# A gated tile moved behind the second pointwise product, and pairs of column sums with more buffers, in a two-block kernel

## What is computed

```python
hl = modulate(rms_norm_2(xl, norm1_g[i]), sh1_l, s1_l)
# conformer_conv(hl, rows, ...):
u = h @ w_pw1 + b_pw1
a, gate = jnp.split(u, 2, axis=-1)
u = a * jax.nn.sigmoid(gate)
u = dwconv(u.reshape(B * n_seg, L // n_seg, D), w_dw).reshape(B, L, D) + b_dw
u = jax.nn.silu(layer_norm(u, ln_g, ln_b))
yl = u @ w_pw2 + b_pw2
# second_block goes on:
xl = xl + g1_l * yl
xl = xl + g2_l * sq_relu_mlp(modulate(rms_norm_2(xl, norm2_g[i]), sh2_l, s2_l), mlp_w1[i], mlp_w2[i])
return rms_norm_2(xl, final_g)
```

## Time and profile before

| what | value |
|---|---|
| three runs | 2130.7, 2130.88 and 2135.11 us, median 2130.88 us |
| the profiled execution's own time | 2129.87 us |
| its span | 2128.1 us |
| PE busy | 2044.6 us (96%), 10322 matmuls, mean granted clock 0.98 |
| DVE busy | 1064.0 us (50%) |
| ACT busy | 814.7 us (38%) |
| POOL busy | 773.2 us (36%) |

### The profile page before, as it was taken

How to read it: one execution, slowest core, us unless ns; L and a number is a source line. 1 busy time by engine, 2 the same in 40 slices (tenths; PEclk the granted TensorE clock), 3 DMA queues, 4 the chain that set the end, 5 groups by cost and what they waited for, 6 DMA issues and landing times. The chain is left out here.

```text
span 2128.1 us, 26521 instructions
## 1 busy us (share of the span) xinstructions
PE 2044.6 (96%) x10322; PEld 1713.7 (81%) x10322; DVE 1064.0 (50%) x1881; ACT 814.7 (38%) x1365; POOL 773.2 (36%) x449
## 2 busy tenths in 40 slices
PE   9999999999999799999899987999999999999997
PEld 7988988988987588888788776778878888888886
DVE  7255445545563456553779969992423221112125
ACT  5533332254335413222456564643335333322311
POOL 3411111121113444344168956753334444222220
PEclk9999999999999899999999998998999999999998
DMA  4301101110113487673344422222233333111112
GB/s 170 108 21 54 47 21 60 41 55 26 46 46 115 164 306 267 226 267 119 109 175 181 178 74 65 83 86 70 79 89 99 95 95 98 50 50 42 48 50 79
DMA packets 69564, 215.64 MB, mean 101 GB/s; under 512 B 7856, under 2 KB 8240, under 8 KB 69312
## 3 DMA queue, kind: packets, MB, share of 16 engines
q1 hardware_dynamic: 55472, 188.26, 26.5%
q10 hardware_dynamic: 13968, 25.70, 3.6%
HBM read 184.56 MB, written 29.36 MB: 101 GB/s over the span
## 5 line engine op out<-in xcount | busy, mean ns | idle before, releaser
L1358 PE MATMUL B<-HB,WH 128*128 128x512 f32 x2976 | 943.7, 403 | 28.1 <-DVE GA L2070 15.6
L2577 POOL TENSOR_TENSOR WL<-RAW,WH 128x1024 fp32r<-128x1024 f32 x205 | 495.5, 2421 | 956.7 <-ACT WH L1755 956.2
L1358 PEld LDWEIGHTS B<-HB,WH 128*128 128x128 f32 x2976 | 552.9, 191 | 150.4 <-issue 19.4
L1358 PE MATMUL B<-HB,WL 128*128 128x512 f32 x1488 | 571.2, 394 | 5.6 <-POOL WL L2577 5.6
L1755 ACT ACTIVATE WH<-RAW 128x1024 fp32r<-128x1024 f32 x205 | 215.6, 1055 | 510.8 <-DMA RAW<-wall 491.6
L1358 PEld LDWEIGHTS B<-HB,WL 128*128 128x128 f32 x1488 | 282.7, 190 | 68.0 <-POOL WL L2577 7.2
L2073 DVE SCALAR_TENSOR_TENSOR RES<-B,modv,RES 128x512 f32<-128x512 f32 x144 | 104.9, 746 | 208.5 <-PE B L1537 182.2
L2073 DVE SCALAR_TENSOR_TENSOR B<-UP,vec,B 128x512 f32<-128x512 f32 x308 | 207.2, 747 | 0.0
L1537 PE MATMUL B<-HIDH,WH 128*128 128x512 f32 x512 | 187.7, 400 | 6.4 <-DVE HIDL L2070 4.9
L1537 PE MATMUL B<-HIDH,WL 128*128 128x512 f32 x512 | 183.6, 392 | 0.0
L1537 PE MATMUL B<-HIDL,WH 128*128 128x512 f32 x512 | 183.4, 391 | 0.0
(11 more groups left out here) (241 smaller groups left out, 2579.1 us busy)
## 6 DMA issues: line engine op xcount, KB each, us to landing
RAW<-wall SPq DMA_DIRECT2D x204, 512.0 KB, 3.5
MODRAW<-wmod ACTq DMA_DIRECT2D x96, 256.0 KB, 4.8
WH<-parts SPq DMA_DIRECT2D x32, 512.0 KB, 3.2
WL<-parts SPq DMA_DIRECT2D x32, 512.0 KB, 4.2
RES<-xT SPq DMA_DIRECT2D x16, 512.0 KB, 8.3
oscr<-OT SPq DMA_DIRECT2D x32, 256.0 KB, 2.1
OI<-oscr SPq DMA_DIRECT2D x16, 512.0 KB, 5.0
parts<-WH SPq DMA_DIRECT2D x16, 512.0 KB, 5.3
```

Source lines behind the costliest of these rows:

```text
L1358: i = pe.matmul(bank, a[:, ks], hb(part, k, h), start=k == 0 and n == 0, stop=k == 7 and n == 2)
L2577: po.tensor_tensor(lo, raw, hi.bitcast(F32), ALU.subtract).then_inc(sig[f"w_lo{q % NW}"], 1)
```

## The change

There are four edits.

1. The last gated tile of half 1, `pa` and `pg` of f = 7, leaves its place before `pw2` of half 0 and comes after it; `before_mlp(0)` now steps in the background of `pg`. The `glu` of (6, 1) and its convolution come after the first layer norm, that of (7, 1) after the MLP's norm, and the POOL convolution of (5, 1) after that.
2. In `normed(0)` the column sums are put on PE two after each group, and all of them count from the first square (`made[0]`). In `normed(1)` one sum is followed by at least one step.
3. The squares have six buffers in half 0 and eight in half 1. `LATE` of half 1 is 14.0 and not 22.0, `LATE_SQ` of half 1 is 6.0 and not 12.0.
4. From the first `ysub` of half 0 to `ln_r` the POOL lane is held, so that no tap stands ahead of the power on POOL.

```diff
-LATE, LATE_SQ, LATE_ROW = (8.0, 22.0), (5.0, 12.0), 5.0
+LATE, LATE_SQ, LATE_ROW = (8.0, 14.0), (5.0, 6.0), 5.0
...
-        for f in range(8):
+        for f in range(8 - h):
             plan += [("pa", f, h), ("pg", f, h)]
...
-    plan += [("pw2", f, 0) for f in range(8)] + mlp[0]
+    plan += [("pw2", f, 0) for f in range(8)] + [("pa", 7, 1), ("pg", 7, 1)] + mlp[0]
...
-            while lanes[lane] and now[lane] < now["pe"] + ahead[0]:
+            while lanes[lane] and now[lane] < now["pe"] + ahead[0] and not (held[0] and lane == "pool"):
...
+        held[0] = h == 0
         for f in range(8):
             piece("ysub", f, h)
             piece("ysq", f, h)
             made.append(now["dve"])
         for f in range(8):
-            yield from until(made[f] + LATE_SQ[h])
+            yield from until(made[f if h else 0] + LATE_SQ[h])
             piece("ysum", f, h)
-            if f % 2:
+            if f % 2 or h:
                 yield
         piece("ln_r", h)
+        held[0] = False
...
+            if (f, h) == (BY_POOL[1][1], 1):
+                piece("glu", f, h)
+            elif (f, h) != (6, 1):
+                convolve(f, h)
...
     hurry[0] = False
+    convolve(6, 1)
...
     second_product(0)
-    beside(before_mlp(0), {0: 1, 1: 1, 2: 1, 3: 1, 4: 1})
+    while not up_free[5]:
+        lanes_step()
+    product("pa", 7, 1)
+    bg.append(before_mlp(0))
+    product("pg", 7, 1)
+    drain()
+    convolve(7, 1)
+    lane_add("pool", conv_pool(BY_POOL[1][1], 1))
     first_hidden(0)
...
-        YT = [[at(f"YT{h}{i}", 512, F32, (x0 + (10 + i) * K2, hb0 + (4 + i) * K4 + K2)[h]) for i in range(4)] for h in range(2)]
+        YT = [[at(f"YT0{i}", 512, F32, x0 + (10 + i) * K2) for i in (0, 1, 2, 3, 6, 7)],
+              [at(f"YT1{i}", 512, F32, hb0 + (4 + i) * K4 + K2) for i in range(8)]]
...
-                if f >= 4:
-                    w.wait_ge(sig["ysum"], nth["ysum", f - 4, h] - h)
-                ac.activation(YT[h][f % 4][:, :], CO[h][f][:, :], ACT.Square).then_inc(sig["ysq"], 1)
+                n = len(YT[h])
+                if f >= n:
+                    w.wait_ge(sig["ysum"], nth["ysum", f - n, h] - h)
+                ac.activation(YT[h][f % n][:, :], CO[h][f][:, :], ACT.Square).then_inc(sig["ysq"], 1)
```

More of the change, by code:

```diff
@@ L183, in make_plan @@
     lanes = {"dve": [], "pool": []}
-    ahead, pace = [AHEAD], [PASS]
+    ahead, pace, held = [AHEAD], [PASS], [False]
     def u_split():
@@ L871, in make_plan, with convolve @@
     piece("a2")
+    def convolve(f, h):
+        piece("glu", f, h)
+        if f in BY_POOL[h]:
+            lane_add("pool", conv_pool(f, h))
+        else:
+            lane_add("dve", conv_dve(f, h))
     for h in range(2):
-        for f in range(8):
+        for f in range(8 - h):
             while not up_free[(8 * h + f) % 10]:
@@ L1633, in ysum @@
                 for t in range(4):
-                    i = pe.matmul(bank[:, t:t + 1], YT[h][f % 4][:, t * 128:(t + 1) * 128], ones[:, 0:1],
+                    i = pe.matmul(bank[:, t:t + 1], YT[h][f % len(YT[h])][:, t * 128:(t + 1) * 128], ones[:, 0:1],
                                   start=f == 0 and t == 0, stop=f == 7, skip_group_check=True)
```

## The result

The changed kernel takes **2115.76 us** (median of 4 runs, 2112.25 to 2117.7) where the kernel before takes 2132.95 in the same session: ratio 0.9927, 95% interval [0.9913, 0.9941]. Five more runs in a later session gave 2116.39 and 0.9937 [0.9925, 0.9949]. By the two ratios it is faster by 13 to 16 us; the forecast was 2126.0 with a range down to 2119, so the direction was right and the size was not. The profiled execution of the changed kernel has a span of 2115.9 us, 12.2 shorter than before.

A forecast was written before the change was run, and what follows sets the result against it. PE was taken as the bound, busy 2044.6 of 2128.1 us, with DVE setting the end of `pw2`. Gains 0.6 + 2.6 + 1.7 = 4.9 us took the profiled 2129.87 to 2125.0, median forecast 2126.0, range 2119 to 2134.

The forecast's parts named there:

- The first layer norm: Half 0's sums: half clock from the third pair, last sum at 1241.8 as before, row at 1247.7, not 1249.23.
- The case of the full clock: Rival: clock holds in half 0's sums, row at 1242.7, 9.8 us gained, 2121.1 us; chance 0.23.
- "slower" rival: Clock falls at half 0's first pair, normalised tiles 4.2 us later; half 1 loses another 5.7; 2135.9 us; chance 0.15.
- The fall at 1478: Clock drop at half 1's sums in the earlier trace, taken as agreeing that frequent micro-idles can lower the clock.
- Normalised tiles, `pw2`, the MLP's norm: Steps after half 0's row: last low part at 1261.6, `pw2` ends 44.5 us later, norm gap 25.4; 2.6 us kept.
- Z: Moment the last low part of half 0's normalised tiles is ready, forecast at 1261.6, 9.7 us earlier than before.
- The first hidden tiles and the stretch to 1394.71: Two terms after the MLP's norm of half 0: 0.6 us left, then 2.6 gained from shrinking waits, bounds 0 and 4.1.
- nothing is left: Rival: POOL's extra taps make low parts late, the 2.6 and 0.6 us go and 1.7 more; 2130.9 us; chance 0.2.
- A: Stretch from the first sum of half 0 to hidden tile 12; forecast gain 3.2 us.
- The layer norm of half 1: Old loss of 8.4 us becomes 6.7 through a 5 us HIDL wait and half clock; 1.7 gained.
- B: Stretch from hidden tile 12 to the row of the MLP's norm of half 1; forecast gain 1.7 us.
- DVE is the last engine at the end of `pw2`: Condition in half 0: DVE ends after PE there, so PE's waits cost nothing; otherwise the prediction is wrong.

The follow-up runs named there:

- again: The changed kernel profiled and timed a second time with no edit; 2116.39 us, ratio 0.9937 to the kernel before.
- yt0_four: The changed kernel with four buffers, not six, for the squares of half 0; 2116.09 us, ratio 0.993 to the kernel before.
- norms_only: The changed kernel without the move of the last gated tile, all edits of both layer norms kept; 2122.67 us, ratio 0.9966 to the kernel before.
- after: The first profile of the changed kernel, nothing else edited; median 2115.76 us, ratio 0.9927 to the kernel before.
- pairs1: The changed kernel with the step after each sum of half 1 taken out, so sums stand adjacent; 2123.92 us, ratio 0.9957 to the kernel before.
- h1_undone: The changed kernel with half 1's layer norm as before (LATE 22, LATE_SQ 12, four buffers, adjacent sums); 2116.76 us, ratio 0.9936 to the kernel before.
- no_hold: The changed kernel without the hold of POOL's taps in half 0's layer norm; 2117.82 us, ratio 0.9937 to the kernel before.
- h1_buffers: The kernel before with eight buffers for the squares of half 1 and nothing else; 2124.47 us, ratio 0.9975.
- late36_single: The kernel before with LATE of half 1 at 36, not 22, and a step after each sum of half 1; 2120.40 us, ratio 0.9959.
- late36: The kernel before with one number changed, LATE of half 1 36 and not 22; 2122.38 us, ratio 0.9969.
- single0: The changed kernel with one sum of half 0 between groups, not two; 2112.46 us, ratio 0.992 to the kernel before; repeated later, 2114.65 us, 0.9933.

## Why the prediction was right and where it was wrong

**The first layer norm.** "I take the fall in the third pair": it fell there in three profiles (again, yt0_four, norms_only) and in the second pair in four (after, pairs1, h1_undone, no_hold). With the fall in the third pair the row is 18.18 us after the first sum; forecast were 17.9. The case of the full clock (row at 12.9) came in none of seven. With the fall in the second pair the last low part of the normalised tiles is 35.3 us after the first sum, 3.4 later than forecast, which is near the 4.2 of the "slower" rival.

The Trainium skill (TensorE: Matmul & The Clock Gate, "A second HAM failure mode: psum-queue depth-cycling") ties such a fall to frequent micro-idles between groups of matmuls. The trace agrees only in that no long gap was needed: in 1231.59 to 1252.97 PE was busy for all 21.38 us, with no idle between groups, and the clock averaged 0.60. The fall at 1478 too, which the prediction counts as agreement, came without an idle in the trace.

**Normalised tiles, `pw2`, the MLP's norm.** Right by their steps: 32.04 us to Z in the second profile where 31.8 were forecast, 44.5 for 44.5, 24.7 for 25.4, and each wait in its place (3.5 for 3, 3.1 for 4 to 5). The 5 us in `pw2` were forecast for WL alone; 2.75 were for WL, and 1.54 before them for DVE. That 44.5 came out to the tenth is in part luck: the terms that the prediction names, 42.9 + 2.0 + 0.75 less one tap of 0.66, make 45.0, and of the 2.0 us of table load and Sigmoid 0.7 had passed before the last low part ended (1266.15 and 1266.86). ACT's table load before (6, 1) took 1.28 us and the Sigmoid came 0.02 behind it. The further 1.38 us that the Trainium skill (ScalarE: Activation LUTs, "What ACT_TABLE_LOAD costs") adds did not appear; the measurement decides, as the sum had it.

**The first hidden tiles and the stretch to 1394.71.** Forecast gains of 0.6 and 2.6. In the second profile the row of the residual's norm, which stands in hidden tile 6, is 132.3 us after the first sum where before has 132.8, so 0.5 gained. From there to hidden tile 12 it is 81.9 for 86.7, 4.7. That is above the bound of 4.1: both waits went whole. The rival "nothing is left" did not come: in 1353.06 to 1400.60 POOL was busy for 44.81 of 47.54 us, but PE waited for nothing. So A gained 5.3 us in the profile with the fall in the third pair, which is the case that was forecast, against 3.2. In the four with the fall in the second pair it gained 2.1 to 2.8. That these lie close to 3.2 is luck: a fall that came early made up for the waits that went whole.

**The layer norm of half 1 is the step that failed.** It said that the squares end 6.4 us after the mean, the hidden tile behind them at 8.9, "and PE reaches the matmul that needs them after 3.6. That is 5 us of waiting". The first half is what happened: the mean at 1469.61, the hidden tile's HIDL at 1478.69, 9.1 later. The second is not: PE waited for nothing between 1471 and 1499. I took the wait for HIDL of the earlier trace rows as a wait for data, and so put the next one at a matmul that reads tile 15. In that place PE reads tiles 8 to 11. The wait before, at 1480.90, was at the first matmul of the second tile of `half_group`, four products after hidden tile 13, for the bank that tile's square and low part had not left. For tile 15 the same point comes 12 groups and two sums after 1471.18, at 1481.10, 2.4 us after HIDL. So 5 us of waiting and 1.7 of half clock behind it were booked that did not exist. With them out the term is 8.4, not 1.7; the 0.98 at the row went too, and B measured 9.1. With 9.1 for 1.7 the sum of 4.9 becomes 12.3. Counted from the first sum the two profiles gained 14.0 and 14.6: the first has 0.6 less in A and 2.4 of scatter behind B, the second 2.1 more in A and 0.3 behind B.

The bounds given for the term were a loss of 4 and a gain of 8. But the range came from the rivals, and all of them spoke of half 0, apart from a second loss in half 1. None let half 1 come out whole, although had the price of that, and the order had the squares ahead of one hidden tile and not of three.

**"DVE is the last engine at the end of `pw2`"** was named as a condition of the prediction, and it holds in the changed kernel: PE ended its last product of `pw2` at about 1308.4, DVE had its last tile done at 1311.35. DVE's chain starts at the last low part of the normalised tiles and follows the row of the norm. So, with the move, A follows the row: rows at 21.4 us give 216.7 to 217.4, at 18.2 they give 214.2 and 214.3, at 15.3 they give 211.7 and 213.4. Without the move PE still waits for DVE's taps further on, and these waits hide it. That is why single sums can be worth something only now.

What stays open: why the clock fell in the second pair in some executions and the third in others, and why it held at adjacent sums of half 1 in h1_undone. How much the single sums and the buffers of half 1 are worth beside the move is not resolved either: the profiles say 2.3 us (129.18 and 126.89), the times nothing. And single sums in half 0 bring the clock back in both profiles of single0, but what that is worth lies between nothing and some 4 us in the times.

## What to carry to other kernels

When a matmul waits for a vector engine, ask whether it waits for what it reads or for the bank it writes. The two put the next wait at different places of the order, and a forecast that mixes them is off by the whole wait. A part of a queue that waits for PE is harmless as long as nothing that PE needs stands behind it: 10 to 12 us of ACT's standing cost 4.3 us behind hidden tile 12 (before against h1_buffers) and at most about 1 us behind tile 15 (late36_single has B 127.88, norms_only with eight buffers 127.04), and one number of the planner was worth half the change (late36, 0.9969). A part of the sum can also come out right for the wrong reason, as A did here; a second profile of the same kernel showed it.

## What the runs showed of the hardware

Adjacent one-column sums took TensorE from 2.4 to 1.2 GHz with the engine never idle, in all seven profiles with four pairs and one group between them. With one sum between groups the clock stayed at 1.00 in all ten that have it in half 0, with as many sums; `single0` differs from the changed kernel in that alone. In half 1, with two or three pairs, it fell in four profiles (before, h1_buffers, pairs1, late36) and held in one (h1_undone), so pairs do not bring the fall every time. "Never idle" means that the trace has no gap between PE's records.

The stretch to the first sum, with the same instructions on PE and DVE, took 1226.2 to 1237.1 us in 17 profiles. A difference of spans between two single profiles is no better than that. Stretches counted from an event of their own can repeat to 0.1 us (B is 126.86 to 126.90 in seven profiles at clock 1.00), but need not: A is 211.72 and 213.44 in the two profiles of single0, and from the row of the MLP's norm of half 1 to the end it is 539.0 to 543.0.
